# Conditioning weights summed by VectorE in three feed-forwards, and none multiplied in the first layer's attention

## The reference

```python
for l in range(DEPTH_2):
    mod_x = (jax.nn.silu(c) @ w_ada[l] + b_ada[l]).reshape(bn, 1, N_MOD, d)
    mod_c = (jax.nn.silu(c_ctx) @ w_ada[l] + b_ada[l]).reshape(1, 1, N_MOD, d)
    h_x = _half_ffn(h_x, norm_g[l, 0], mod_x[:, :, 0], mod_x[:, :, 1], mod_x[:, :, 2], ffn1_up[l], ffn1_down[l])
    ...
```

## Time and profile before

| | us |
|---|---|
| median of 3 runs | 2215.75 |
| lowest, highest | 2213.92, 2223.4 |
| the profiled execution, its own time | 2216.32 |
| its span in the trace | 2215.0 |
| mean granted clock of TensorE | 0.978 of full |

### The profile page before, as it was taken

The page is one execution under the profiler, slowest core; times in us unless marked ns, Lnnn a source line. Parts: engine busy times, 40 slices in busy tenths (PEclk is TensorE's granted clock), DMA queues, the critical chain, the costliest instruction groups (busy, mean ns, idle before and its releaser), DMA issues. The chain is left out here.

```text
span 2215.0 us, 41069 instructions
## 1 busy us (share of the span) xinstructions
PE 2140.7 (97%) x17886; PEld 1844.7 (83%) x17886; DVE 1074.3 (49%) x1570; ACT 770.6 (35%) x1094; POOL 60.3 (3%) x59
## 2 busy tenths in 40 slices
PE   7998899999999999989999999999999999899998
PEld 7887699998888888867788888888888888779998
DVE  5654765565333335676453333354333335755555
ACT  5331444453222223236332222233222223355433
POOL 0000030000000000220000000000000000200000
PEclk9998899999999999999999999999999999999999
DMA  7516644543323224337422232232232225254543
GB/s 283 198 63 236 240 175 164 195 173 115 147 90 116 95 78 127 91 117 285 172 99 94 84 114 95 79 140 78 89 109 95 83 97 153 96 193 168 174 174 111
DMA packets 56627, 303.57 MB, mean 137 GB/s; under 512 B 13728, under 2 KB 17184, under 8 KB 27552
## 3 DMA queue, kind: packets, MB, share of 16 engines
q1 hardware_dynamic: 56480, 301.40, 38.8%
HBM read 300.33 MB, written 1.05 MB: 136 GB/s over the span
## 5 line engine op out<-in xcount | busy, mean ns | idle before, releaser
L459 PE MATMUL ps<-a_hi,w_hi 128*128 128x512 f32 (+1 forms) x1992 | 683.5, 343 | 1.7 <-DVE w_lo L446 1.5
L460 PE MATMUL ps<-a_lo,w_hi 128*128 128x512 f32 (+1 forms) x1992 | 678.0, 340 | 0.0
L461 PE MATMUL ps<-a_hi,w_lo 128*128 128x512 f32 (+1 forms) x1992 | 677.8, 340 | 0.0
L446 DVE TENSOR_TENSOR w_lo<-raw,w_hi 128x2048 fp32r<-128x2048 f32 (+2 forms) x230 | 470.1, 2047 | 207.7 <-ACT w_hi L440 207.4
L440 ACT ACTIVATE w_hi<-raw 128x2048 fp32r<-128x2048 f32 (+2 forms) x229 | 391.2, 1715 | 234.2 <-PE ps L461 174.3
L459 PEld LDWEIGHTS ps<-a_hi,w_hi 128*128 128x128 f32 x1992 | 377.8, 190 | 47.9 <-issue 3.6
L461 PEld LDWEIGHTS ps<-a_hi,w_lo 128*128 128x128 f32 x1992 | 378.0, 190 | 42.2
L460 PEld LDWEIGHTS ps<-a_lo,w_hi 128*128 128x128 f32 x1992 | 378.0, 190 | 41.8
L459 PE MATMUL ps<-ff_hi,w_hi 128*128 128x512 f32 (+1 forms) x880 | 306.5, 348 | 3.6 <-DVE w_lo L446 3.2
L460 PE MATMUL ps<-ff_lo,w_hi 128*128 128x512 f32 (+1 forms) x880 | 304.9, 347 | 0.0
L461 PE MATMUL ps<-ff_hi,w_lo 128*128 128x512 f32 (+1 forms) x880 | 304.9, 346 | 0.0
(11 more groups left out here) (356 smaller groups left out, 1829.4 us busy)
## 6 DMA issues: line engine op xcount, KB each, us to landing
raw<-in_w_gu SPq DMA_DIRECT2D x110, 1024.0 KB, 4.8
raw<-in_w_ada SPq DMA_DIRECT2D x72, 1024.0 KB, 5.2
raw<-in_w_dn SPq DMA_DIRECT2D x80, 704.0 KB, 4.0
raw<-in_w_in SPq DMA_DIRECT2D x26, 1024.0 KB, 4.9
raw<-in_w_out SPq DMA_DIRECT2D x12, 1024.0 KB, 5.4
direct<-in_w_cmp SPq DMA_DIRECT2D x4, 1024.0 KB, 6.9
h<-in_x SPq DMA_DIRECT2D x2, 1024.0 KB, 7.1
nb<-in_rpb SPq DMA_DIRECT2D x32, 64.0 KB, 7.4
```

What stands on the lines that cost most here:

```text
L446: nc.vector.tensor_tensor(w_lo[slot][:, cols], raw[b][:, cols], w_hi[slot][:, cols].bitcast(F32), ALU.subtract).then_inc(lo_ready if done ...
L459: nc.tensor.matmul(banks[m], w1, a1, start=start and k == 0, stop=False)
L460: nc.tensor.matmul(banks[m], w1, a2, start=False, stop=False)
L461: last = nc.tensor.matmul(banks[m], w2, a1, start=False, stop=stop and k == pr.kt - 1)
```

## The change

36 of the 72 chunks are handled in another way and at other places. A *part* is now two neighbouring chunks (512 features) of which one half of the rows is loaded, again 1 MB. VectorE multiplies its four row blocks by the two conditioning vectors and sums them: eight operations of 512 elements for a part, into the buffer `gu` of the chunk after this one and, in place, into the part's own first block. This happens in the body of chunk k for the part that stands before chunk k + 2. TensorE sums over the partitions with `fold_ada`: eight matmuls with a stationary `pick` whose used column is ones, streaming 128 columns, after the twelfth matmul of chunk k + 1. Two parts (both halves of the rows) add up in one bank and are drained together.

There are 6 parts in the first and 8 in the second half of `w_gu1_0` and of `w_gu2_0`, and 8 in the second half of `w_gu1_1`: 36. The 24 chunks in layer 0's attention, the 8 in `pe_first` and the 4 streamed ones are gone. `with_mods` computes the vectors derived from the modulation in two feed-forwards more.

```diff
-BATCHES = [(0, 5, 3), (5, 7, 3), (12, 8, 6)]
-EARLY = 20
-INNER = {"w_out": (1, 8), "w_out_0": (2, 24), "w_out_1": (2, 10), "w_gu": (2, 1), "w_gu1_0": (2, 1), "w_in_0": (2, 1),
+BATCHES = [(0, 5, 3), (5, 7, 3)]
+EARLY = 12
+INNER = {"w_out": (1, 8), "w_out_1": (2, 10), "w_gu": (2, 1), "w_gu1_0": (2, 1), "w_in_0": (2, 1),
          "w_gu2_0": (2, 1), "w_gu1_1": (2, 1), "w_in_1": (2, 1)}
+STREAM = {"w_gu1_0": (6, 8), "w_gu2_0": (6, 8), "w_gu1_1": (0, 8)}
+STREAM_AT = 2
...
+    ada_beside = {pr.ada(k): gu[(pr.base + k - 1) % RING] for pr in products for k in pr.ada_at}
...
+    def fold_ada(pe, a, b):
+
+        part = streamed.index(a) % 2
+        if part == 0:
+            pe.wait_ge(ada_drained, a)
+        pe.wait_ge(ada_summed, summed(a) + KT)
+        for w in range(2):
+            for g in range(4):
+                c = slice(32 * g, 32 * (g + 1))
+                at = (by_rows(ada_slot[a], 0) if w else ada_sum(a)).rearrange("p u (m f) -> p u m f", m=2)
+                last = nc.tensor.matmul(b[c].rearrange("p (u m f) -> p u m f", u=2, m=2), pick[:, w, :],
+                                        at[:, :, :, c], start=part == 0 and w == 0, stop=part == 1 and w == 1,
+                                        tile_position=(0, 32 * g))
+        last.then_inc(ada_mult, 1)
+
+    def sum_ada(dve, pr, k):
+
+        a = pr.ada(k)
+        turn, slot = pr.loaded(k, 0, 1)
+        n = summed(a)
+        dve.wait_ge(landed[slot], 16 * (turn + 1))
+        for j in range(HEAD_K):
+            x = by_rows(slot, j)
+            for w, to in enumerate((ada_sum(a), by_rows(slot, 0))):
+                c = silu_c[:, HEAD_K * (streamed.index(a) % 2) + j, w:w + 1]
+                wait(dve, ada_summed, n - (1 if j else 0))
+                if j:
+                    last = nc.vector.scalar_tensor_tensor(to, x, c, to, ALU.mult, ALU.add)
+                else:
+                    last = nc.vector.tensor_scalar(to, x, c, None, ALU.mult)
+                last.then_inc(ada_summed, 1)
+                n += 1
...
     def stream_drain(dve, a):
-        drain_ada(dve, a, 1, ps[6][:, 0:64])
+        drain_ada(dve, a, 2, ps[6][:, 0:P])
...
-            if first + k in pr.ada_at:
-                pe.wait_ge(ada_drained, pr.ada(first + k))
-                multiply_ada(pe, pr.loaded(first + k, 0, 1), ps[6][:, 0:64])
+            if first + k + 1 in pr.ada_at:
+                before = lambda m, j: (m, j) == (0, HEAD_K) and fold_ada(pe, pr.ada(first + k + 1), ps[6][:, 0:P])
             multiply(pe, pr, c, slot, [bank(slot, m, t) for m in range(pr.mt)], lhs, rhs, before=before)
...
             if k or pr.name not in ("w_out_0", "w_out_1"):
                 split(c + 1, pr.loaded(head + k + 1, r), (slot + 1) % RING, pr.size)
+            if evac_ada is not None and k + 2 in pr.ada_at:
+                sum_ada(eng, pr, k + 2)
```

More of the change, by code:

```diff
@@ L233, in add, with streams @@
         n_ada[0] += len(ada_at) + out[-1].inner[1]
+    def streams(name, half):
+        return range(STREAM_AT, STREAM_AT + STREAM.get(name, (0, 0))[half])
     def add_gu(name, tokens, half, ada_at=()):
@@ L249, in plan @@
         for half in range(2):
-            add_gu(f"w_gu1_{l}", T2, half, range(4) if l == 0 and half == 0 else ())
+            add_gu(f"w_gu1_{l}", T2, half, streams(f"w_gu1_{l}", half))
             add(f"w_dn1_{l}", KT, FH, 1, T2, "down", half * KT)
@@ L255, in plan @@
         for half in range(2):
-            add_gu(f"w_gu2_{l}", t, half)
+            add_gu(f"w_gu2_{l}", t, half, streams(f"w_gu2_{l}", half))
             add(f"w_dn2_{l}", KT, FH, 1, t, "down", half * KT)
@@ L410, in program, with ada_sum, by_rows @@
     products = plan()
+    streamed = [pr.ada(k) for pr in products for k in pr.ada_at]
+    ada_slot = {pr.ada(k): pr.loaded(k, 0, 1)[1] for pr in products for k in pr.ada_at}
+    ada_beside = {pr.ada(k): gu[(pr.base + k - 1) % RING] for pr in products for k in pr.ada_at}
+    def ada_sum(a):
+        return ada_beside[a][:].rearrange("p (u f) -> p u f", u=2)
+    def by_rows(slot, j):
+        return raw[slot][:].rearrange("p (u k f) -> p u k f", u=2, k=HEAD_K)[:, :, j, :]
     gu_before = {}
@@ L490, in multiply_ada, with summed @@
         last.then_inc(ada_mult, 1)
+    def summed(a):
+        return KT * streamed.index(a)
+    def fold_ada(pe, a, b):
[27 more added lines that the diff above has]
+                n += 1
     turned = [0]
@@ L664, in staged @@
         c = pr.end - 1
-        if pr.n - 1 in pr.ada_at and evac_ada is not None:
-            evac_ada(pr.ada(pr.n - 1))
+        if evac_ada is not None and pr.ada_at:
+            evac_ada(pr.n - 1)
         if pr.ahead is not None:
@@ L800, in evac @@
             last.then_inc(chunk_drained, 1)
-            if pr.inner[1] and pr.kind == "res" and i == 1:
+            if pr.kind == "res" and i == 1:
                 key = attend_key(pr)
@@ L818, in dve_product, with stream @@
             dve.wait_ge(sq_cleared, norm_serial(pr.squares) + 1)
+        def stream(k):
+            if k in pr.ada_at and streamed.index(pr.ada(k)) % 2:
+                stream_drain(dve, pr.ada(k) - 1)
         if pr.name == "w_out":
             dve.wait_ge(lo_ready, pr.base + 1)
-        staged(dve, pr, split, evac, chained[pr.base], lambda a: stream_drain(dve, a))
+        staged(dve, pr, split, evac, chained[pr.base], stream)
     squared = {pr.squares: pr for pr in products if pr.squares is not None}
@@ L1081, in program @@
     vct = place("vct", [P, 2, HD], F32)
+    pick = place("pick", [P, 2, 32], F32)
     at_rope = cursor[0]
@@ L1893, in pe_attend @@
                 scores(j0 + t, jobs[t])
[L1894 to L1897, removed]
+            if key != "first" and t == 3:
+                pe.wait_ge(pr_dve, qd(key, "pool"))
+                pe.wait_ge(pr_act, qa(key, "pool"))
+            if 3 <= t < inner_count(key) + 3:
                 if t % 2:
@@ L2410, in load @@
                     free(k, r, 1)
-                    b = pr.loaded(k, r, 1)[1]
-                    sp.dma_start(raw[b][:], dram["w_ada"][pr.ada(k)]).then_inc(landed[b], 16)
+                    b, a = pr.loaded(k, r, 1)[1], pr.ada(k)
+                    part = streamed.index(a) % 2
+                    sp.dma_start(raw[b][:].rearrange("p (u x) -> p u x", u=2),
+                                 dram["w_ada"][a - part:a - part + 2].rearrange("u p x -> p u x")
+                                 [:, :, CH // 2 * part:CH // 2 * (part + 1)]).then_inc(landed[b], 16)
                 free(k, r, 0)
@@ L2510, in _ @@
         nc.vector.memset(silu_c[:], 0.0).then_inc(silu_c_cleared, 1)
+        step(nc.vector.memset(pick[:], 0.0))
+        for w in range(2):
+            last = nc.vector.memset(pick[:, w, w:w + 1], 1.0)
+        step(last)
         dve.wait_ge(consts_loaded, 32)
@@ L2536, in _ @@
             elif kind == "mods":
-                dve_mods(dve, step, x, (0, 1))
+                dve_mods(dve, step, *x)
             elif kind == "meet":
```

23 lines of the change are left out of this document (11 added, 12 removed).

## The result

The changed kernel took 2232.86 us (median of 7 runs, 2227.2 to 2235.99) against 2215.02 us for the kernel before (7 runs, 2208.86 to 2223.4): a ratio of 1.0073, 95% interval 1.0052 to 1.0093, by which it is some 16 us slower (the medians are 17.8 apart). The forecast was 2224.0, range 2209 to 2242. The range holds the result, but the likeliest case, within 0.5%, did not come; slower by over that had 0.37. The profiled execution has a span of 2231.8 us against 2215.0, 16.8 more, and that is split up here. Lines moved: 488 of before is 506 after, 446 is 464, 459 to 461 are 477 to 479, 498 and 501 are 553 and 556, 759 is 819, 1864, 1872 and 1883 are 1929, 1937 and 1948, 1975 is 2040.

What follows compares the result with a forecast made beforehand. TensorE, busy 97% of the span, was taken as the bound. Folds +26.3, drain waits +8.2, attention -19.9, streamed parts -5.0, early parts -1.9 make +7.7 us on 2216.32: 2224.0, range 2209 to 2242.

Steps and rivals of the forecast that it cites:

- the likeliest case: Whole kernel: within 0.5% (11 us) of the kernel before, chance 0.54; the forecast's own case, 2224, had 0.50.
- 0.73 each: Gate/up: each fold costs TensorE 0.52 us of passes plus 0.22 of entering and leaving; 26.3 us added for 36.
- 13 waits at the drain: Gate/up: a pair's first fold waits 0.63 us for the last pair's drain of their shared bank; 8.2 us added.
- attention of layer 0, to the next gate product: First layer's attention: without its 24 parts VectorE and ScalarE become the bound; 19.9 us saved, between 14 and 29.
- before the first block's attention: Eight parts there mostly fill TensorE's waits; removing them saves 1.9 us, or nothing if the attention starts at low clock.
- costed at nothing: Extra modulation vectors, memsets at the start, unrolled loops and half-row loads in 4 KB pieces: 0 us.
- the half-width pair: First layer's attention: two half-width jobs take 4.95 us without parts; four pairs took 25.8 us before, 6.0 saved.
- The 10.3 us of the mixed steps: First layer's attention: the four mixed steps go from 13.5 us to 10.3 without parts, 3.2 saved.
- VectorE falls behind: Rival, slower: gate/up sums take 7.2 us without overlap and delay the gate product; some 35 us more, 2255, chance 0.12.
- That even job takes VectorE 2.41 us: First layer's attention: VectorE's share of a full-width pair of 7.1 us, 8.28 before; four pairs save 4.7 us.
- gives back less: Rival, slower: the attention's chain has a missed link between its engines; 10 us given back, 2234, chance 0.12.
- the clock falls: Rival, slower: idler TensorE drops to 1.2 GHz in the attention, 12 jobs lose 13 us; 2237, chance 0.10.

Runs made afterwards that it cites:

- the pair above: The pair-wise sums with eight old parts back before the first block's attention (28 folded parts), against the pair-wise sums of 36 parts: 2208.54 and 2213.27 us.
- the pair-wise sums: Changed kernel with VectorE summing both parts of a pair and one fold a pair behind the eighteenth matmul: 2212.75 us, 0.9995; repeated unchanged, 2213.27 us, 1.0001.

## Why the prediction was right or wrong

| term | forecast | the profile's |
|---|---|---|
| 36 folds | +26.3 (0.73 each) | +30.2 (0.84 each) |
| 13 waits at the drain | +8.2 (0.63) | +8.1 (0.62) |
| four old streamed parts | -5.0 | -5.0 |
| attention of layer 0, to the next gate product | -19.9 | -17.7 |
| before the first block's attention | -1.9 | -0.4 |
| costed at nothing | 0 | +1.7 |
| sum | +7.7 | +16.9 |

**Right in kind.** The range holds the time, but in part by luck: its upper end was set for the rivals of the attention, and what used it up were smaller errors elsewhere. Of the likeliest case these came: the new wait with its length, place and count; the sums hidden, 4.97 us instead of 5.1, with 1.35 us left instead of 1.0; loads in time (no chunk is longer than its fold and its wait explain); the half-width pair at 4.95. Three workings are looser than they look. ScalarE's 1.65 us in that pair is 1.75 to the copy's end by the earlier trace rows; after the change the next exponential starts 1.63 behind (1046.89 to 1048.52), since neighbours overlap. The 10.3 us of the mixed steps come without rows. The 35 us of *VectorE falls behind* are 38 by their own terms (36 x 0.7 and 13 x 1), so 2262 and not 2255. *VectorE falls behind* did not come, and its margin held even for the longer sums of a pair.

**"0.73 each" for a fold** is the step that failed most, 3.9 of the 9.2 us. The passes were scaled by columns from a part of 64 passes and the edges taken as the 0.22 of a part. The old part has the same 0.32 ahead of it and the same 0.34 behind (579.69 to 580.01, 581.04 to 581.38). But where the part's 64 passes took 1.03 us, the fold's two sets take 0.57, not 0.52, and the product's steps behind a fold stay at 0.23 to 0.24 for longer. Neither the place nor the sums beside it make the difference (both were tried); why a short group pays more than its share is open. The Trainium skill's figure ("TensorE: Matmul & The Clock Gate", Part 3, measured speedup, 3.07 for four) is of row groups, and this kernel packs columns. The 0.67 us of passes drawn from it would have given, as an estimate, 0.89 a fold, nearer the 0.84, but for a reason that the runs don't bear out: passes measure 0.39 to 0.51 us for sixteen.

**The attention** gave 17.7 instead of 19.9, and over ten profiles without parts 16.3 on the mean. By step, it was for the first part nothing instead of 1.0, full-width pairs 2.4 instead of 4.7, mixed 3.0 instead of 3.2, half width 5.6 instead of 6.0, tail 5.9 instead of 5.0, and 0.9 behind it, in the projection, norm and gate/up head that follow. "That even job takes VectorE 2.41 us" left out the wait of 0.46 to 0.69 for scores: with parts TensorE ran ahead there, and without them its own order (value product, then scores) is a link of the chain in every second pair. That is the rival *gives back less* at a small size. The first pair, 8.1 us, ran partly at 1.2 GHz. By the Trainium skill (same page, Part 1) the low clock is the default and recent activity lifts it; the trace agrees at the attention's start, where TensorE had waited, and behind it TensorE, busy 85% of the time, kept 0.99; so *the clock falls* came for one pair instead of twelve jobs.

**The eight parts before the first attention** gave nothing that can be seen, where 1.9 was forecast. The bound from below, nothing, was the right value, and the two profiles agree with its reason. TensorE's first scores of that attention and its next ones behind a wait, before, then after:

```profile
227.71 0.34 PE L1864 MATMUL ps<-p 64*128 64x128 f32 x1 [1.84 <-DVEq L2358]
231.99 0.58 PE L1864 MATMUL ps<-p 64*128 64x128 f32 x1 [1.96 <-ACT ee L1920]
```

```profile
226.76 0.55 PE L1929 MATMUL ps<-p 64*128 64x128 f32 x1 [0.91 <-DVEq L2419]
231.56 0.58 PE L1929 MATMUL ps<-p 64*128 64x128 f32 x1 [1.86 <-ACT ee L1985]
```

The start is 0.95 us earlier, the very price of the drain, but the next step only 0.43. From 220 to 230 the mean granted clock is 0.50, where it was 0.75 before; TensorE was busy for 6.63 of those 10 us against 7.05, and for 4.08 against 8.90 of the 10 ahead of them. All profiles lean that way: up to the first gate product TensorE runs at 1.2 GHz for 44 to 58 us in the eight without the parts, for 21 to 44 in the six with them. That this is what eats the saving fits, but no run holds the clock and takes the parts alone.

**At nothing** stood also the stretch from the second layer's first feed-forward to its second. It took 237.4 us before and 239.0 after. In the busy time by window, before and after, the same place (TensorE always busy, clock third from the end):

```profile
1892.50:1896.00 3.50, 3.50 (x17) 2.87 (x17) 3.43 (x4) 0.28 (x1) 3.26 (x4) 1.00 0.00 0
```

```profile
1908.50:1912.00 3.50, 3.50 (x12) 2.76 (x11) 3.41 (x4) 0.28 (x1) 3.23 (x4) 0.64 0.00 0
```

In the changed kernel the granted clock fell to half for 3.4 us from 1907.6 on, behind a norm's matmuls of two columns and into a projection, without any wait; before, the same matmuls led to no fall. Eight profiles with 12 early parts have 237.4 to 240.5 us there (mean 239.5), six with 20 have 236.1 to 237.4 (mean 236.7). That also is where the 4.7 us of the pair above exceed the 3.4 of the folds. What goes with the length is the time at 1.2 GHz in this stretch: 10.2 to 13.7 us in the seven profiles of 236.1 to 237.4, 17.1 in the three of 239.0 to 239.2, 20.5 in the four of 240.2 to 240.5. The +1.7 is thus one more fall (17.1 against 13.7 us). One of the seven has 12 early parts, so they don't decide it alone, and no run tells why they should matter 1600 us later.

**What failed in the chances**: four errors of size all fell to one side, and nothing in the sum allowed for that; it stood at +7.7 with the bound of "slower" at 11, so 0.07 for that from the likeliest case was too little.

## What to carry to other kernels

A group of small matmuls put between large ones is paid by the group more than by its passes: merge groups (one fold for two parts took 15 us off the chunks) before shortening them. Filler in a stage bound by other engines can be cheap at first and dear later (here 0.4 us each of 1.03 up to one a pair of steps, 0.9 each beyond), so take out the second half of it, not all. A wait that is the difference of two near-equal times goes when its consumer stands a few matmuls later; a drain moved to idle time can come back as a wait of the next writer of its bank.

## What the runs showed of the hardware

- Sixteen passes of 128 columns in four column groups cost 0.84 us in the midst of products, the next sixteen 0.39; a set of four groups steps by 0.22 to 0.24, and the product's matmuls behind take 0.23 to 0.24 instead of 0.227 for some ten steps.
- The granted clock fell to half for 3.4 us with TensorE busy all the time (1907.6 of the changed kernel), and such falls stand in other places in other programs. In the two stretches counted above, another 3.4 us at 1.2 GHz goes with some 1.2 to 1.7 us more. Gate/up chunks of one kind without a drain agree to 0.02 us in all profiles. Two profiles of one program (the pair-wise sums) are 1.25 us apart at the first gate product, 1.6 around layer 0's attention and 2.9 around layer 1's, all in stretches with such falls (23.9 against 20.5 us at 1.2 GHz in the second stretch, 13.7 against 20.5 in the third).
- Multiply-adds of 512 elements that wait only for the one before the last step by 0.66 us at a length of 0.75.
